# A fused decoder step: order of work in the first expert, one weight load in halves, and the place of the down bias

## What is computed

```python
logits = h @ w_router + b_router
top_val, top_idx = lax.top_k(logits, TOP_K)      # 4 of 32
gates = softmax(top_val)
# for the rows of expert e:
gt = jnp.minimum(xe @ w_gate[e] + b_gate[e], 7.0)
up = jnp.clip(xe @ w_up[e] + b_up[e], -7.0, 7.0)
yb = ((up + 1.0) * gt * sigmoid(1.702 * gt)) @ w_down[e] + b_down[e]
x = x + sum over the four experts of gate * yb
```

## Time and profile before

| | us |
|---|---|
| median of 3 runs | 1165.84 (1164.99 to 1166.95) |
| the profiled execution | 1165.45 |
| its span, first to last instruction | 1163.6 |
| TensorE busy in it | 1122.2 |
| VectorE busy | 529.1 |
| ScalarE busy | 212.3 |
| read from HBM | 424.92 MB |

### The profile page before, as it was taken

How to read it: one execution, slowest core, us unless ns; L and a number is a source line. 1 busy time by engine, 2 the same in 40 slices (tenths; PEclk the granted TensorE clock), 3 DMA queues, 4 the chain that set the end, 5 groups by cost and what they waited for, 6 DMA issues and landing times.

```text
span 1163.6 us, 16613 instructions
## 1 busy us (share of the span) xinstructions
PE 1122.2 (96%) x6608; PEld 480.4 (41%) x6608; DVE 529.1 (45%) x1123; ACT 212.3 (18%) x433; POOL 34.1 (3%) x47
## 2 busy tenths in 40 slices
PE   9999999999999999999999999999999999999997
PEld 7666786643333333333333333333333333333332
DVE  6999965337333333333333333333333333333333
ACT  3265642221111111111111111111111111110012
POOL 0002412000000000000000000000000000000000
PEclk9999999999999999999999999999999999999999
DMA  9724006999999999999999999999999999999995
GB/s 247 214 86 179 20 16 175 429 392 415 417 427 427 429 428 430 427 429 427 430 429 427 430 427 430 428 429 427 430 427 429 430 426 430 429 429 427 429 421 204
DMA packets 58587, 430.00 MB, mean 370 GB/s; under 512 B 16670, under 2 KB 29390, under 8 KB 34220
## 3 DMA queue, kind: packets, MB, share of 16 engines
q1 hardware_dynamic: 58288, 428.84, 89.7%
q10 hardware_dynamic: 260, 0.61, 0.2%
HBM read 424.92 MB, written 4.48 MB: 369 GB/s over the span
## 4 chain that ended last, share of the span: by engine, by line
PE 53%; DMA 29%; DVE 4%; issue 1%; ACT 1%; DVEq 0%; ACTq 0%
PE bank L2166 35%; DMA ring<-in_w_up_dram 26%; PE bank L2133 5%; DMA arena<-in_w_up_dram 3%; PE bank L2140 2%; PE bank L2086 2%; PE bank L1734 2%; DVE arena L2536 1%; DVE arena L2560 1%; PE bank L1312 1%; PE bank L1271 1%; PE bank L2174 1%; PE bank L2192 1%; PE bank L1320 0%; PE bank L278 0%
## 5 line engine op out<-in xcount | busy, mean ns | idle before, releaser
L2166 PE MATMUL bank<-arena 128*64 128x512 f32 x1540 | 344.2, 594 | 11.4 <-DMA arena<-in_w_up_dram 11.2
L2166 PE MATMUL bank<-ring,arena 128*64 128x512 f32 x1532 | 342.2, 594 | 11.8 <-DMA ring<-in_w_up_dram 11.0
L2166 PEld LDWEIGHTS bank<-arena 128*64 128x64 f32 x1540 | 108.0, 136 | 225.8 <-issue 197.9
L2166 PEld LDWEIGHTS bank<-ring,arena 128*64 128x64 f32 x1532 | 108.0, 137 | 225.2 <-issue 198.0
L2560 DVE TENSOR_TENSOR arena<-arena,bank 128x512 f32<-128x512 f32 x180 | 110.0, 680 | 0.0
L2549 DVE SCALAR_TENSOR_TENSOR arena<-bank,arena 128x512 f32<-128x512 f32 x31 | 23.3, 751 | 182.0 <-ACT arena L1928 182.0
L2536 DVE TENSOR_SCALAR arena<-bank 128x512 f32<-128x512 f32 x31 | 21.4, 692 | 179.9 <-PE bank L2174 179.9
L610 PE MATMUL bank<-arena,ring 128*128 128x336 f32 x352 | 102.5, 447 | 0.3 <-DVE arena L751 0.3
L2133 PE MATMUL bank<-arena 128*64 128x512 f32 x372 | 86.7, 599 | 4.3 <-DVE arena L2560 0.6
L1904 ACT COPY arena<-bank 128x512 f32<-128x512 f32 x31 | 18.2, 587 | 354.3 <-PE bank L2133 354.3
L610 PEld LDWEIGHTS bank<-arena,ring 128*128 128x128 f32 x352 | 65.8, 189 | 34.2 <-issue 2.9
(11 more groups left out here) (387 smaller groups left out, 785.5 us busy)
## 6 DMA issues: line engine op xcount, KB each, us to landing
ring<-in_w_gate_dram SPq DMA_DIRECT2D x32, 2048.0 KB, 29.8
arena<-in_w_up_dram SPq DMA_DIRECT2D x32, 2048.0 KB, 32.8
arena<-in_w_gate_dram SPq DMA_DIRECT2D x32, 2048.0 KB, 29.9
arena<-in_w_down_dram SPq DMA_DIRECT2D x31, 2048.0 KB, 35.4
ring<-in_w_down_dram SPq DMA_DIRECT2D x31, 2048.0 KB, 35.4
ring<-in_w_up_dram SPq DMA_DIRECT2D x29, 2048.0 KB, 32.9
ring<-in_w_in_dram SPq DMA_DIRECT2D x11, 1024.0 KB, 8.4
ring<-in_w_up_dram SPq DMA_DIRECT2D x11, 512.0 KB, 7.3
```

The source lines that it names most:

```text
L2166: mm = M.matmul(bank[64 * hb:64 * hb + 64, b, :], tokens(cc), rows[:, 512 * hb:512 * hb + 512], start=(cc == 0), stop=(w3 == 2 and cc == K ...
```

## The change

- ScalarE, first expert: the turned activations are copied ahead of the gathered rows.
- TensorE, first expert: the down units no longer wait behind the turn of the gathered rows and that of the gates. The turn of the gathered rows is put between the two down units, and the turn of the gates after both.
- SP: the 13th unit, which takes the slot of the 5th (the first down unit of the first expert), is loaded in halves. The first half is issued when half of the 5th unit has been used.
- The product of gates and `b_down` is put into `combine` in the body of the 31st expert (the last but one) instead of the second. The wait for `gt_ready` stays in the second expert.

```diff
@@ SP
                 for k in range(NSLOT + 2, PER):
+                    if k == NSLOT + 4:
+                        w = unit_src(k // EU, k % EU)
+                        sp.wait_ge(first_half, 1)
+                        sp.dma_start(unit_tile(k)[:, 0:2, :], w[:, 0:2, :]).then_inc(half_landed, 16)
+                        sp.wait_ge(unit_used, UPRE + k - NSLOT + 1)
+                        sp.dma_start(unit_tile(k)[:, 2:4, :], w[:, 2:4, :]).then_inc(landed[k % NSLOT], 16)
+                        continue
                     sp.wait_ge(unit_used, UPRE + k - NSLOT + 1)
                     start_unit(sp, k // EU, k)
@@ ScalarE body
-                    take_rows(at(1, 3))
-                    take_act(at)
                     if first:
+                        take_act(at)
+                        take_rows(at(1, 3))
                         act.wait_ge(F["gt_turned"], 1)
                         A.copy(gT32, bank[:, 6, 0:NT]).then_inc(F["gt_ready"], 1)
+                    else:
+                        take_rows(at(1, 3))
+                        take_act(at)
                     take_down(at)
@@ TensorE product
                     for u in range(2):
+                        if u and between:
+                            between()
...
+                            if first and k == 4 and c == 2:
+                                mm.then_inc(first_half, 1)
-                            if first and cc == 2:
+                            if first and w3 == 0 and cc == 2:
                                 pe.wait_ge(F["x_ready"], 2)
@@ TensorE combine
                     if biased:
-                        pe.wait_ge(F["gt_ready"], 1)
                         pe.wait_ge(F["bdown_in"], 16 * 4)
@@ TensorE body
-                        combine(before, biased=second)
+                        if second:
+                            pe.wait_ge(F["gt_ready"], 1)
+                        combine(before, biased=late)
...
                     turn_p(at)
-                    pe.wait_ge(F["xg_ready"], at(1, 3))
-                    turn(xg, 5).then_inc(F["x_done"], 1)
+
+                    def turn_next():
+                        pe.wait_ge(F["xg_ready"], at(1, 3))
+                        turn(xg, 5).then_inc(F["x_done"], 1)
+
                     if first:
+                        down(at, over, first=True, between=turn_next)
                         for k in range(6):
                             ...
                         mm.then_inc(F["gt_turned"], 1)
-                    if not first:
+                    else:
+                        turn_next()
                         pe.wait_ge(F["cmb_read"], before(6, 4))
-                    down(at, over)
+                        down(at, over)
@@ TensorE, order of the bodies
                     body(0, r, first=(r == 0), second=(r == 1))
+                pe.wait_ge(half_landed, 16)
                 with pe.Fori(0, NGROUP - 1) as it:
                     ...
                 for r in range(PEEL, GROUP - 1):
-                    body(NGROUP - 1, r)
+                    body(NGROUP - 1, r, late=True)
                 last_body()
```

More of the change, by code:

```diff
@@ L1689, in build @@
         early_landed = lsem("early_landed")
+        first_half = lsem("first_half")
+        half_landed = lsem("half_landed")
         PIECES = {PER - 3: 4, PER - 2: 2, PER - 1: 4}
@@ L2141, in turn, with product @@
                     return mm
-                def product(at, k0, b, tokens, w3, over, final=False, first=False, early=False):
+                def product(at, k0, b, tokens, w3, over, final=False, first=False, early=False, between=None):
                     for u in range(2):
+                        if u and between:
+                            between()
                         k = EU * over[0] + k0 + u
@@ L2201, in gate_up, with down @@
                             early=early).then_inc(F["u_done"], 1)
-                def down(at, over, final=False):
+                def down(at, over, final=False, first=False, between=None):
                     if final:
@@ L2208, in down @@
                         pe.wait_ge(F["aT_ready"], at(1, 1))
-                    product(at, 4, 2, lambda cc: aT[:, cc % 4, cc // 4, :], 2, over, final)
+                    product(at, 4, 2, lambda cc: aT[:, cc % 4, cc // 4, :], 2, over, final, first=first, between=between)
                 def add_last(i):
@@ L2280, in last_body, with body @@
                     add_last(2)
-                def body(it, r, first=False, second=False):
+                def body(it, r, first=False, second=False, late=False):
                     at = counter(it, GROUP, r)
```

## The result

| | before | after |
|---|---|---|
| median, us | 1164.87 (10 runs) | 1167.34 (10 runs) |
| lowest to highest | 1163.07 to 1166.95 | 1165.14 to 1168.69 |
| the profiled execution | 1165.45 | 1165.78 |
| its span | 1163.6 | 1164.0 |

The ratio is 1.0020, with a 95% interval of 1.0012 to 1.0028: slower by 2.5 us in the medians. The two profiled executions differ by only 0.3 us, because the one before lies in the upper third of its kernel's executions and the one after is nearly the fastest of its ten; the profile after must not be read as if it showed the median. The change was to work at three places, and each is seen there.

The account below looks back on a forecast made before the run. The load stream, set by the 19th unit's issue, then TensorE's chain at the end were taken to bound the kernel. +0.95 (later 19th unit) and +1.6 (late bias) gave +2.5 us: 1168.3, range 1165.9 to 1169.7.

Parts of the forecast that it names:

- The first expert: First expert: down units 0.54 us earlier, first half issued 2.5 ahead, y1 and VectorE's split 0.95 later.
- the copies' order alone gives nothing: First expert, ScalarE: swapping the two copies by itself gives 0.05 us at most.
- VectorE holds the second gather: Second expert: the gather waits for VectorE's first add, so removing 1.91 us of bias products gains nothing; gather at 283.6.
- Rival 1: Second expert: the gather follows TensorE, 19th unit issued at 288.5, total 1165.4 us; chance 0.08.
- The late bias: 31st expert: bias behind TensorE's wait delays the last up units and the end by 1.6 us (1.3 to 1.8).
- The room that I took from one row: Last expert's first up unit: TensorE was ready 0.15 to 0.19 us before its load landed; 0.19 taken off 1.78.
- Rival 3: Kernel's end: TensorE makes up the late bias's 1.6 us, leaving +0.95, total 1166.8 us; chance 0.08.
- Term one: Second expert: the 19th unit is issued 0.95 us later, at 291.5, and the stream behind it is 0.95 later.
- the issue of the 19th unit sets the stream: Load stream, hole at 292: its last hole hangs on this issue at 290.57; moving it moves the end.
- Rival 2: Load stream: the first hole's 1.4 us gain at 260 is kept, total 1166.0 us; chance 0.10.
- Rival 4: TensorE's 3.0 us pause before the second gather: the clock halves, up to 7.9 us more, total 1172; chance 0.03.
- My price of 4: Second expert: half of the up to 7.9 us that a clock fall in TensorE's pause could add, giving 1172.

Follow-up runs that it names:

- late bias alone: Kernel before with only the down bias moved from the second to the 31st expert: 1166.55 us against 1164.22.
- gates first: Changed kernel with the turn of the gates put back ahead of the down units: 1166.74 us against 1164.22 for the kernel before.
- table split: Changed kernel, gates' turn before down units, bias in third expert, end of VectorE's overflow table after second: 1163.69, again 1163.55 us, against 1164.42 before.
- bias back: Changed kernel with the down bias returned to the second expert: 1164.33 us against 1164.22 for the kernel before, ratio 1.0006.
- gates first as well: Changed kernel with the bias returned to the second expert and the gates' turn ahead of the down units: 1164.41 us against 1164.42 for the kernel before.
- halves alone: Kernel before with only the 13th unit's load in halves: 1164.64 us against 1164.42, ratio 1.0003; run a second time, ratio 0.9992.
- after again: Changed kernel without any edit, run and traced a second time: 1167.38 us against 1164.22 for the kernel before.
- filling the pause alone: Changed kernel with five unread products in TensorE's pause ahead of the second gather: 1165.71 us against 1164.42 for the kernel before.

## Why the prediction was right, and where it was not

The time was right, 1167.3 within 1165.9 to 1169.7 and +2.5 us as forecast, but the sum behind it was right in only one of its two terms, and that one came out a little below its range. A mechanism that I gave 3 in 100 makes up for what was over-counted: that the total fits is in part luck.

**The first expert: right.** Down units at 256.30 (forecast 256.27), the first half at 258.28 (258.1), y1 at 265.09 (264.95), the split at 265.81 (265.7). That the copies' order alone gives nothing is seen in L1931, which starts at 255.66, as late as before.

**VectorE holds the second gather: right, and shown.** The gather did not move when 1.9 us of products ahead of it were taken out (late bias alone), came 0.7 earlier when y1 did (gates first), and followed TensorE at once when the table was moved (table split). Rival 1 has fallen.

**The late bias: right in place, a little too dear.** Forecast +1.6 (1.3 to 1.8), and TensorE's way to the last up units is 1.5 longer. Of that the end pays 1.2: leg 3 is 30.73 to 31.14 in the five traces with the bias behind the wait, 30.87 on average, and 29.51 to 29.89 in the eight without it, 29.63. The room that I took from one row, 0.19, was too small: from the last up bias to the next start I counted 0.32, and in the trace of after it is 1134.46 - 1134.24 = 0.22. The wait for that load is 0.25 with the bias back and 0.68 with the gates first as well. Rival 3 has fallen: the end swallows at most a quarter of it.

**Term one: the issue was right, what follows from it was not.** The 19th unit came 1.05 later (forecast 0.95). The step that failed is "the issue of the 19th unit sets the stream". In the traces where the 19th unit is late, leg 2 is 841.3 to 841.8 and the end follows it. Before, leg 2 is 843.4 and 843.9: there the end hung on the slowest of the 16 DMA engines, which had work left when the others ran dry at 292. In the first trace the last increment of the 18th unit came at 295.25, 4.7 after the 19th had been issued, and that of the 19th 5.19 later, where one unit takes 4.9 in the full stream; for the median engine it was 5.59. The rows that I read show the sum over all engines, and a sum hides that. A wider hole lets the slow engine come up with the others (its lag after the 19th unit is 2.5 in the trace of before, 0.6 in that of after), and so takes back what it costs. In the two profiles of the change it took back all of it, if they are set against the two of before; but about 1.5 of each of those two lags is the step beside an instruction packet, and without it the lag would have been 1.6 to 1.8, near that of the other kernels. At the 36th unit, ahead of these steps, the lag is 2.2 and 2.4 before and 1.6 and 1.5 after, so 0.6 to 0.8 of the 1.05 had come back there. How much of it comes back in a usual execution is not shown. The medians leave it open too: with the bias back, where this term stands alone, the ratio of 1.0006 (0.9997 to 1.0014) allows for anything from -0.3 to +1.6 us.

**Rival 2, the kept gain of the first hole, did not show.** With the halves alone the median engine's leg 2 is 839.7 and 840.0, before it is 840.1 and 840.7, where a kept gain would be 1.4. Of the two ratios, the first excludes -1.4 us and the second does not.

**Rival 4 came true.** The clock fell after TensorE's pause in three of the four executions profiled with a pause of 2.5 to 2.7 us, and in none of the others there. It cost 1.45 (late bias alone), 1.61 (gates first) and 1.73 us (after again) on leg 1. My price of 4 was too high, and the chance far too low: I had held against it that after the last product the clock stayed up for 3.3 us, one fall in one place. The Trainium skill (TensorE: Matmul & The Clock Gate, Part 1) gives idle stretches as the cause of the halved clock; the traces agree with that. Pauses of 2.50, 2.51 and 2.66 us were enough here, shorter than the gaps that the Trainium skill warns of in the same part, and one of 2.63 was not.

Together, in the trace of the kernel after with the fall: leg 1 +2.75 (1.03 through y1, 1.7 through the clock), leg 2 -2.1 to -2.6, leg 3 +0.8 to +1.1. That is +1.0 to +1.7 against the two traces of before. The medians say +2.5 and +3.2. The difference is that both traces of the kernel before lie in the upper part of its spread: their executions took 1165.45 and 1166.15, and of all 121 executions of this kernel on record, with a median of 1164.5, 76% and 94% were faster. So in a usual execution of the kernel before the lag, and with it leg 2, must be smaller than in the two that were profiled; the step of 1.5 at an instruction packet, which each of the two has, is about as much as is missing. This is worked out and not seen. As an estimate for a usual execution: 1.05 for the 19th unit, less 0.7 that comes back, 1.2 for the tail, and 1.7 for the clock in the 13 of the 20 executions of the kernel after whose mean clock is 0.997 or less, is 1.05 - 0.7 + 1.2 + 1.1 = +2.7 us.

By parts, from runs beside each other: taking the bias back takes off 3.05 us (tail and clock together), filling the pause alone brings the ratio from 1.0020 and 1.0029 to 1.0011, moving the gates ahead takes off 0.6, which is not clear of noise.

## What to carry to other kernels

Work that is taken off a waiting engine does not make it earlier, it only makes the wait longer, and a longer wait of TensorE can lower its clock for the work that the wait was for; before moving products out of such a place, ask what ends the wait, and leave them there if it is another engine. Slack has a place: TensorE waited 1.25 us in the 31st expert, but ahead of the bias and not behind it, and the same six products cost 1.2 us behind that wait and 0.3 in front of it. And a load is there when the slowest DMA engine has done its sixteenth, so a stream's holes are to be read by engine where the trace allows it, not from the bandwidth of all.

## What the runs showed of the hardware

- The last of a load's 16 landings can run 1.0 to 3.5 us behind the median one, and the lag stays for hundreds of us of a full stream: in the first trace of before it was 3.54 at the 46th, the 66th and the 176th unit. It shrinks where the others have nothing to do (from 2.17 to 0.59 over the hole at 292 in the trace of after).
- In that stream the lag rises beside packets of the instruction queue: 16 KB that take 1.10 us, and 1.08 instead of 0.61 for the packet behind, with a step of 1.55 in each of the two traces of before.
- The granted clock fell to 1.2 GHz for 3.41 us in the executions named, beginning now before and now after TensorE's work had gone on (at 283.51 with the gather at 283.31, 284.07 with 283.02, 282.41 with 282.83). The same pause of the same code brought a fall in one execution and none in another.
